# The first two tiles of each output projection woven chunk by chunk into the last attention unit and the last stick-breaking head

## What is computed

```
# layer 1: sliding-window attention with sinks, 32 heads of 64, 4 key heads
q, k, v, gate = split(rms_norm(x) @ w_in1);  q, k = rms_norm(q), rms_norm(k)
o  = softmax_with_sink(q k^T / 8 + bias, band of 128) v
x1 = x + (o * silu(gate)) @ w_out1
# layer 2: 8 stick-breaking heads (sb) and 8 differential heads (df), 16 meta tokens in front
sb_q, sb_k, sb_v, sb_g, df_q, df_k, df_v, df_g = split(rms_norm([meta; x1]) @ w_in2)
sb = exp(log_sigmoid(z) + reverse_cumsum(log_sigmoid(-z))) v * silu(sb_g)
df = rms_norm((softmax_1 - lam * softmax_2) v) * (1 - lam_init) * silu(df_g)
out = x1 + [sb, df] @ w_out2
```

## Time and profile before

| | us |
|---|---|
| median of three runs | 1877.64 (1875.6 to 1878.66) |
| the profiled execution | 1878.74 |
| its span, first to last instruction | 1877.0 |
| PE busy | 1833.1 (98%) |
| DVE busy | 936.7 (50%) |
| ACT busy | 868.4 (46%) |
| L480 on PE in the chain that ended last | 78% of the span |

### The profile page before, as it was taken

The page is one execution under the profiler, slowest core; times in us unless marked ns, Lnnn a source line. Parts: engine busy times, 40 slices in busy tenths (PEclk is TensorE's granted clock), DMA queues, the critical chain, the costliest instruction groups (busy, mean ns, idle before and its releaser), DMA issues.

```text
span 1877.0 us, 28406 instructions
## 1 busy us (share of the span) xinstructions
PE 1833.1 (98%) x9917; PEld 1546.1 (82%) x9917; DVE 936.7 (50%) x2320; ACT 868.4 (46%) x2026; POOL 36.9 (2%) x65
## 2 busy tenths in 40 slices
PE   7899999999998999999999999999999999979999
PEld 5688888888876888898888988889888888958887
DVE  5356565565655333554545646454564645544221
ACT  4356666565655322443534445353544534453221
POOL 1000000000001000000000000000000000000000
PEclk9999999999998999999999999999999999979999
DMA  7922222222215444332222213222222222214442
GB/s 188 224 73 83 80 81 74 80 81 82 80 34 142 129 138 139 102 87 79 71 80 80 78 57 91 78 71 77 80 73 73 81 78 70 67 33 129 135 134 84
DMA packets 297107, 173.47 MB, mean 92 GB/s; under 512 B 22880, under 2 KB 285616, under 8 KB 297024
## 3 DMA queue, kind: packets, MB, share of 16 engines
q1 hardware_dynamic: 290256, 151.28, 28.6%
q0 software_dynamic: 5696, 20.25, 4.5%
q10 hardware_dynamic: 1088, 1.08, 0.3%
HBM read 156.86 MB, written 14.66 MB: 91 GB/s over the span
## 4 chain that ended last, share of the span: by engine, by line
PE 94%; DMA 2%; DVE 1%; ACT 1%; SPq 0%; issue 0%; ACTq 0%; DVEq 0%
PE G L480 78%; DMA raw<-in_swa_w_in 2%; PE G L601 1%; PE O L841 1%; PE S L812 1%; PE S L766 1%; PE O L601 1%; PE O L784 1%; PE G L588 1%; PE S L578 1%; PE S L577 1%; PE T L588 1%; PE G L728 1%; PE G L563 1%; PE S L830 1%; PE S L827 0%
## 5 line engine op out<-in xcount | busy, mean ns | idle before, releaser
L480 PE MATMUL G<-xh,wh 128*128 128x512 f32 (+1 forms) x2624 | 891.6, 371 | 8.0 <-DVE xl L1562 4.9
L480 PE MATMUL G<-xl,wh 128*128 128x512 f32 (+1 forms) x2624 | 844.7, 354 | 0.0
L480 PE MATMUL G<-xh,wl 128*128 128x512 f32 (+1 forms) x2624 | 841.3, 352 | 0.0
L480 PEld LDWEIGHTS G<-xh,wh 128*128 128x128 f32 x2624 | 465.0, 189 | 91.4 <-issue 22.5
L480 PEld LDWEIGHTS G<-xh,wl 128*128 128x128 f32 x2624 | 461.8, 189 | 70.2
L480 PEld LDWEIGHTS G<-xl,wh 128*128 128x128 f32 x2624 | 461.8, 189 | 63.3 <-issue 4.8
L1377 DVE TENSOR_TENSOR wl<-raw,wh 128x512 fp32r<-128x512 f32 x528 | 354.2, 688 | 305.5 <-ACT wh L918 301.6
L918 ACT ACTIVATE wh<-raw 128x512 fp32r<-128x512 f32 x528 | 315.5, 620 | 127.5 <-PE G L480 102.0
L1252 ACT ACTIVATE att<-att,st 128x144 f32<-128x144 f32 (+3 forms) x64 | 36.9, 577 | 128.9 <-DVE wmeta L1771 70.3
L1015 ACT ACTIVATE p<-S,rq 128x256 f32<-128x256 f32 (+1 forms) x128 | 50.2, 444 | 47.8 <-PE S L578 46.3
L1478 DVE TENSOR_TENSOR st<-st 128x1 f32<-128x1 f32 x128 | 20.3, 159 | 87.7 <-ACT st L1027 87.7
(11 more groups left out here) (240 smaller groups left out, 1731.8 us busy)
## 6 DMA issues: line engine op xcount, KB each, us to landing
raw<-in_w_in SPq DMA_DIRECT2D x112, 512.0 KB, 4.0
raw<-in_swa_w_in SPq DMA_DIRECT2D x72, 512.0 KB, 4.0
raw<-in_swa_w_out SPq DMA_DIRECT2D x32, 512.0 KB, 5.1
raw<-in_w_out SPq DMA_DIRECT2D x32, 512.0 KB, 4.7
raw<-in_w_in POOLq DMA_DIRECT2D x8, 1024.0 KB, 8.1
rel_rows<-relb POOLq DMA_DIRECT2D x1, 6128.0 KB, 38.4
mixed<-in_x SPq DMA_DIRECT2D x4, 1024.0 KB, 8.7
bias<-rel_rows POOLq DMA_DIRECT2D x16, 256.0 KB, 3.3
```

Source lines behind the costliest of these rows:

```text
L480: mm = pe.matmul(d, w[:, slot, k, :], v[:, k, a:b], start=(k == 0 and n == 0), stop=(k == KC - 1 and n == 2))
```

## The change

In both layers the first two tiles of the output projection become one woven piece, `out1_front` and `out2_front`. Its order is `front_order`: (0,0), then for n = 1 to 11 the product of tile 0 with chunk n and of tile 1 with chunk n-1, then the last four of tile 0 and the last five of tile 1. The chunk that the unfinished attention writes comes last: in layer 1 it is chunk 15 anyway, in layer 2 `FRONT2` puts chunk 7 at the end. Steps 8 to 15 of the last unit, and 0 to 27 of the last sb head, stand between the products. On ACT and DVE the chunk copies run two chunks ahead of PE's place, mixed with those steps and with the four weight splits of tile 1 (`QUARTER_AT`); each copy waits for `chunk_free`, which the last tile before now counts per chunk. The last sb gate's finish moves from the end of the loop to the top of the next round, and for the last head to n = 2. SP's waits before the first residual tiles are loosened (`kv_v` and `q_stat` for `a_out`, `v_t` for `b_out`), its loads for tiles 2 and 3 are written before the first two stores, and two output transposes go to tile 2.

```diff
+        LATE = N2 - 1
+        FRONT2 = [c for c in range(KC) if c != LATE] + [LATE]
+        PAIRED = 12
+        SWA_REST = {1: 8, 2: 9, 3: 10, 5: 11, 6: 12, 8: 13, 9: 14, 10: 15}
+        QUARTER_AT = {0: 0, 2: 1, 6: 2, 9: 3}
+
+        def front_order():
+
+            yield 0, 0
+            for n in range(1, PAIRED):
+                yield 0, n
+                yield 1, n - 1
+            for half in range(2):
+                for n in range(PAIRED - half, KC):
+                    yield half, n
+
...
-                with sp.Fori(1, KC // 2) as i:
+                for half in range(2):
+                    weights(first + 2 + half, half, w_v, P * (2 + half))
+                for half in range(2):
+                    residual(2 + half, 1, half)
+                for half in range(2):
+                    store(half, half)
+                with sp.Fori(2, KC // 2) as i:
                     for half in range(2):
                         tile(i, half)
                         store(2 * i + half - 2, half)
 
             def x_tile(c, i, half):
                 if isinstance(c, int) and c == 0:
-                    sp.wait_ge(a_out, 8 * UNITS)
+                    sp.wait_ge(kv_v, KV)
+                if isinstance(c, int) and c == 1:
+                    sp.wait_ge(q_stat, 4 * UNITS)
...
                 if isinstance(c, int) and c == 0:
                     sp.wait_ge(d_out, N2)
-                    sp.wait_ge(b_out, N2)
+                    sp.wait_ge(v_t, 2 * N2)
...
+            def product(dst, slot, k, cols, first, last, chunk_done=None):
...
-                    product(dst, slot, k, cols, k == KC - 1, chunk_done)
...
+                gemm(T_UNIT + 2 * u + 1, 1, [G[:, 1, :]], PLAIN, lambda p: swa_step(u, g, p),
+                     chunk_done=chunk_free if u == 4 * UNITS - 1 else None)
...
-            for m in range(8, 16):
-                swa_step(4 * UNITS - 1, 3, m)
-
 
...
+                if isinstance(c, int) and c == 0:
+                    pe.wait_ge(a_pT, 4 * 4 * UNITS)
...
+            def out1_front():
+
+                pe.wait_ge(q_lo, 2 * 4 * UNITS)
+                pe.wait_ge(q_sq, 4 * UNITS)
+                for half, n in front_order():
+                    if half and n == 0:
+                        pe.wait_ge(g_ev, 4 * UNITS)
+                    if n % QTR == 0:
+                        pe.wait_ge(w_lo, 4 * (T_OUT1 + half) + n // QTR + 1)
+                    pe.wait_ge(split_lo, n + 1)
+                    product([G[:, half, :]], half, n, PLAIN, n == 0, n == KC - 1)
+                    if half == 0 and n in SWA_REST:
+                        swa_step(4 * UNITS - 1, 3, SWA_REST[n])
+                    if half == 0 and n in (PAIRED, PAIRED + 2):
+                        x_transpose((n - PAIRED) // 2, (n - PAIRED) // 2)
...
-                gemm(T_OUT1 + c, half, [G[:, half, :]], PLAIN, at_point,
-                     (lambda k: pe.wait_ge(split_lo, k + 1)) if first else None, chunk_free if last else None)
-
-            for i in range(2):
-                for half in range(2):
-                    out1_tile(i, half)
+                gemm(T_OUT1 + c, half, [G[:, half, :]], PLAIN, at_point, None, chunk_free if last else None)
...
+            out1_front()
+            for half in range(2):
+                out1_tile(1, half)
...
+            def out2_front():
+                pe.wait_ge(used["sbk"], N2)
+                pe.wait_ge(used["sbv"], N2)
+                pe.wait_ge(d_ln, N2)
+                bank = [G[:, 0, :]], [G[:, 1, :]]
+                sb_step(N2 - 1, 0)
+                sb_step(N2 - 1, 1)
+                for half, n in front_order():
+                    k = FRONT2[n]
+                    if n in (0, 4, 7, 11):
+                        pe.wait_ge(w_lo, 4 * (T_OUT2 + half) + k // QTR + 1)
+                    pe.wait_ge(split_lo, KC + n + 1)
+                    product(bank[half], half, k, PLAIN, n == 0, n == KC - 1)
+                    m = 2 * n + 2 + 3 * half
+                    if m < 28 and (n < PAIRED - half or half == 0):
+                        sb_step(N2 - 1, m)
+                    if half == 0 and n in (0, PAIRED):
+                        sb_step(N2 - 1, m + 1)
...
-                    if p == 2 and not first:
+                    if isinstance(c, int) and c == 2 and p in (2, 6):
+                        out_transpose(p // 4, p // 4)
+                    elif p == 2:
                         out_transpose(c - 1, 1 - half)
...
+                         chunk_free if ti == len(TILES2) - 1 else None)
...
-            for m in range(32):
-                sb_step(N2 - 1, m)
             out2_block()
...
-            for m in range(8, 16):
-                swa_step(4 * UNITS - 1, 3, m)
-
-
-            def mixed_hi():
-                for c in range(KC):
-                    A(xh[:, c, META:ALL], mixed[:, c, :], ACT.Copy).then_inc(split_hi, 1)
+
+            def mixed_hi(c):
+                A(xh[:, c, META:ALL], mixed[:, c, :], ACT.Copy).then_inc(split_hi, 1)
+
+            def out1_front():
+
+                def chunk(c):
+                    act.wait_ge(chunk_free, c + 1)
+                    act.wait_ge(a_out, 2 * (4 * UNITS - 1))
+                    mixed_hi(c)
+
+                chunk(0)
+                chunk(1)
+                for n in range(KC - 2):
+                    if n in QUARTER_AT:
+                        split(T_OUT1 // 2, 1, QUARTER_AT[n], out_loaded(OUT1_LOADS, 0, 1))
+                    if n + 2 < KC - 1:
+                        chunk(n + 2)
+                    if n in SWA_REST:
+                        swa_step(4 * UNITS - 1, 3, SWA_REST[n])
+                act.wait_ge(tile_done, T_OUT1)
+                act.wait_ge(a_out, 8 * UNITS)
+                mixed_hi(KC - 1)
+                for half in range(2):
+                    x_column(half, half)
+                for quarter in range(4):
+                    split(T_OUT1 // 2 + 1, 0, quarter, out_loaded(OUT1_LOADS, 1, 0))
+                x1_square(0, 0)
...
@@ -1316,6 +1380,8 @@
                     for p in range(POINTS):
                         if ti:
                             finish(h, ti - 1, p)
+                        elif attend:
+                            finish(h - 1, len(TILES2) - 1, p)
...
-            for m in range(32):
-                sb_step(N2 - 1, m)
+
+            def out2_front():
+
+                def chunk(n):
+                    act.wait_ge(chunk_free, (KC - 1) * (N2 + 1) + FRONT2[n] + 1) if FRONT2[n] < KC - 1 else act.wait_ge(
+                        tile_done, T_OUT2)
+                    act.wait_ge(d_out, N2)
+                    mixed_hi(FRONT2[n])
+
+                chunk(0)
+                chunk(1)
+                sb_step(N2 - 1, 0)
+                sb_step(N2 - 1, 1)
+                for n in range(KC - 2):
+                    if n in QUARTER_AT:
+                        split(T_OUT2 // 2, 1, QUARTER_AT[n], out_loaded(OUT2_LOADS, 0, 1))
+                    if n + 2 < KC - 1:
+                        chunk(n + 2)
+                    if n == 2:
+                        finish(N2 - 1, len(TILES2) - 1, 0)
+                    for m in (2 * n + 2, 2 * n + 3):
+                        if m < 28:
+                            sb_step(N2 - 1, m)
+                act.wait_ge(b_out, N2)
+                mixed_hi(LATE)
+                for quarter in range(4):
+                    split(T_OUT2 // 2 + 1, 0, quarter, out_loaded(OUT2_LOADS, 1, 0))
...
+                else:
+                    if isinstance(i, int) and i == 1:
+                        out2_copy(0, 0, 0)
                     out2_copy(2 * i - 1, i - 1, 1)
...
-            for m in range(8, 16):
-                swa_step(UNITS - 1, 4 * UNITS - 1, 3, m)
-
...
+            def mixed_lo(c, count):
+                dve.wait_ge(split_hi, count)
+                V.tensor_tensor(xl[:, c, META:ALL], mixed[:, c, :], xh[:, c, META:ALL].bitcast(F32),
+                                ALU.subtract).then_inc(split_lo, 1)
+
+            def out1_front():
+                mixed_lo(0, 1)
+                mixed_lo(1, 2)
+                for n in range(KC - 2):
+                    if n in QUARTER_AT:
+                        split(T_OUT1 // 2, 1, QUARTER_AT[n])
+                    if n + 2 < KC - 1:
+                        mixed_lo(n + 2, n + 3)
+                    if n in SWA_REST:
+                        swa_step(UNITS - 1, 4 * UNITS - 1, 3, SWA_REST[n])
+                mixed_lo(KC - 1, KC)
+                for quarter in range(4):
+                    split(T_OUT1 // 2 + 1, 0, quarter)
+                x1_add(0, 0)
+                x1_squares(0, 0)
+                x1_add(1, 1)
...
-            for m in range(32):
-                sb_step(N2 - 1, m)
-            mixed_lo(KC)
...
+                def chunk(n):
+                    mixed_lo(FRONT2[n], KC + n + 1)
+
...
+                    if n == 2:
+                        finish(N2 - 1, len(TILES2) - 1, 0)
...
+                mixed_lo(LATE, 2 * KC)
```

(4 more changed lines are left out.)

81 lines of the change are left out of this document (32 added, 49 removed).

## The result

The changed kernel takes 1867.94 us (median of 5 runs, 1866.97 to 1868.79) against 1877.64; the ratio is 0.9947, its 95% interval 0.9934 to 0.9959. It is faster by 9.7 us, and the forecast was 1864.7 in a range of 1860.5 to 1871.0. Its profiled execution took 1867.94 too, with a span of 1866.3, which is 10.7 less than before.

What follows compares the result with a forecast made beforehand. PE bounds the kernel, losing time only where it idles or runs at the lower clock in two stretches. Savings 3.9 + 9.0 = 12.9 take 1878.74 to 1865.8, or 1864.7 from the median; range 1860.5 to 1871.

Steps and rivals of the forecast that it cites:

- The third tiles: Start of the third output tile of each layer: 600.5 for 604.43, and 1700.6 for 1710.05.
- Stretch 1: Tail of the last attention unit and first products of its output projection, 560.50 to 578.39: 3.9 us saved.
- the wait for G1: First pair, third product: PE waits 1.7 us until DVE empties bank G1 at 569.4.
- The walk with the clock up: First pair, queue by queue, if the clock never falls: ends at 598.5, 5.9 us saved.
- Stretch 2: Tail of the last stick-breaking head and first products of its output projection, 1656.55 to 1684.62: 9.0 us saved.
- For the clock I add 1.1: Second pair: 1.1 us added, mean of walks with the clock falling at 1659.6, 1663 or again at 1670.
- the walk's 1699.5 without the clock: Second pair, queue by queue before the clock's addition: bank G0 emptied and third tile ready at 1699.5.
- The two new stops: Second pair's head: PE waits 3.3 us for tile 117's late weights, then about 3.4 behind the gate's finish.
- The C steps: Five chain steps of the last stick-breaking head: 4.9, 6.3, 6.3 us apart; PE waits 0.8, 0.8, 1.8, 2.0.
- The rule against the change: PE takes matmuls in order, so each interleaved step stops all products behind; otherwise second pair ends some 6 us earlier.
- The slower rival: Both pairs: the lower clock holds throughout, making the kernel slower at 1896 us; chance 4%.

Runs made afterwards that it cites:

- after_again: The changed kernel run once more with the same code, nothing changed: median 1867.42 us, ratio to the kernel before 0.9932 to 0.9959.
- fillers: The changed kernel plus matmuls that compute nothing ahead of PE's four longest waits: median 1865.79 us.

## Why the prediction was right, and by how much it missed

**The third tiles.** Stretch 1: forecast 600.5, measured 600.83 or 600.3 on the scale of before. The idle time ahead of the first product is 3.61 (forecast 3.8), the wait for G1 1.29 (1.7); with 0.53 taken off, the block-1 transpose comes at 572.0 (572.9) and the clock is low until 573.3 (575). The saving is 4.1 for 3.9. The walk with the clock up ended at 598.5; after_again, whose short dip lies between the two waits, has its third tile at 599.18, which is 598.5 with its own offset of 557.67 - 556.98 = 0.69 taken off. Stretch 2: 1702.4 for 1700.6; 7.6 saved for 9.0, less a longer third tile.

**The term that was mis-sized is the clock in the second pair.** "For the clock I add 1.1" is the mean of walks in which it falls at 1659.6, 1663 or again at 1670. There were three dips, and the third, behind C4, was in none of the walks; it alone costs 1.6 of the 2.8 us between the changed kernel and fillers. Taken off the measured third tile, 1702.4 - 2.8 = 1699.6, against the walk's 1699.5 without the clock. That this comes to 0.1 us is partly luck: the terms below are off by 0.5 to 1.4 us both ways, and from C4 to the third tile the walk counted 11.3 us where fillers, without a dip, takes 11.9 (1682.29 to 1694.19). With the same second pair the load and the dips alone moved B from 46.19 to 47.59.

**The two new stops.** Both were where the prediction put them, for its reasons. The first is 3.77 for 3.3, since the load took 4.8 us to land (1652.25 to the split at 1657.09), not 4.2. The second is 2.05 for 3.4 to 3.5: the gate's finish starts when forecast, 1662.81 + 3.71 = 1666.5 for 1665.9, but PE, late at (1,0) and then at the lower clock, got there only at 1663.6 + 3.71 = 1667.3 instead of 1665.1. The value step itself is at 1669.4 for 1668.6. The C steps stand 5.1, 6.2 and 6.1 us apart for 4.9, 6.3 and 6.3; the waits before them were over-estimated (1.39 for 2.0 at C4, 0.58 for 1.8 at C3).

**The sum.** By the cuts of the table the first pair saved 1097.54 - 1093.30 = 4.24 and the second 222.48 - 215.49 = 6.99 (in which the longer third tile is counted, 0.6 for 0.4), together 11.2 for 12.9; the start took 0.5 more, which gives the 10.7 between the spans. So of the 3.2 us between forecast and median, the second pair explains 2.0 and the start 0.5, the first pair takes 0.3 off, and 1.1 is the step from the profiled execution to the median: the one of before lay 1.1 above its median, that of the changed kernel on it (and in after_again 1.5 below). That step says nothing of the kernel, and it should have stood in the sum with an uncertainty of its own.

**The rule against the change** held: PE takes matmuls in order, and each stop of a step is a stop of every product behind it. **The slower rival**, a low clock through both pairs, did not come: it is low for some 10 us and for some 10 us in three pieces, and at full level in the dense parts between. The Trainium skill's failure mode of short idles that keep bringing the clock down (TensorE: Matmul & The Clock Gate, A second HAM failure mode: psum-queue depth-cycling) is seen in part only: one idle of 1.39 us was followed by 3.4 us at the lower level, and the full level came back by itself.

## What to carry to other kernels

When a chain of short steps is woven into a dense stream of matmuls, list every wait that the stream now stands behind, and look at its head first: a DMA behind another one's wait in a queue, a chain of functions in one piece, a bank that is still full; here these were worth as much again as the weaving itself (13.5 us for 9.7 by the medians, 10.9 for 11.2 by the traces). Keep enough products for the steps, since the early copies without the second tile gave a quarter of the gain by the medians, two fifths by the traces. And count a low clock only where PE would be busy and does not wait behind it.
